# The order of Strassen splits, and two weight splits on GpSimd, in a two-block fp32 network on one core

## The reference

```python
x = x + 0.5 * swiglu(rmsnorm(x, ffn1_norm[l]), ffn1_w_gate[l], ffn1_w_up[l], ffn1_w_down[l])
...  # gated MLP with spatial gating beside a gated delta rule, w_out
x = x + 0.5 * swiglu(rmsnorm(x, ffn2_norm[l]), ffn2_w_gate[l], ffn2_w_up[l], ffn2_w_down[l])
...
def swiglu(x, w_gate, w_up, w_down):
    return (jax.nn.silu(x @ w_gate) * (x @ w_up)) @ w_down
```

## Time and profile before

| | |
|---|---|
| median of 3 runs | 1359.53 us (1359.14 to 1364.18) |
| the profiled execution | 1361.13 us, its span 1359.3 us |
| TensorE matmul busy | 1326.7 us (98% of the span) |
| VectorE, ScalarE, GpSimd busy | 930.1, 814.2, 493.7 us |
| mean granted clock of TensorE | 0.991 |

### The profile page before, as it was taken

One profiled execution on the slowest core, in us unless ns is written; L12 is line 12 of the kernel. 1 busy time (PEld: TensorE's weight loads), 2 busy tenths in 40 slices (PEclk: granted clock), 3 DMA queues, 4 the chain that ended last, 5 costly groups with the idle time before them and its releaser, 6 DMA issues.

```text
span 1359.3 us, 18294 instructions
## 1 busy us (share of the span) xinstructions
PE 1326.7 (98%) x7252; PEld 1113.8 (82%) x7252; DVE 930.1 (68%) x1162; ACT 814.2 (60%) x1095; POOL 493.7 (36%) x220
## 2 busy tenths in 40 slices
PE   9998999999999999999999999999999999999897
PEld 8887777888887888887888887788888888888786
DVE  6778886955577896687886559754335632567887
ACT  7646467456654557655567787667434654654663
POOL 1623213473641504532314231035525524462320
PEclk9999999999999999998999999999999999999999
DMA  9587884234568796577784645355854544648783
GB/s 342 187 211 249 236 288 154 97 97 164 204 163 232 217 266 227 185 183 253 203 289 155 229 175 194 121 182 177 290 183 155 198 143 148 208 156 212 242 211 109
DMA packets 42279, 269.66 MB, mean 198 GB/s; under 512 B 6321, under 2 KB 6865, under 8 KB 11217
## 3 DMA queue, kind: packets, MB, share of 16 engines
q1 hardware_dynamic: 35680, 226.69, 47.5%
q0 software_dynamic: 4608, 33.56, 13.1%
q10 hardware_dynamic: 1904, 8.23, 1.7%
HBM read 267.38 MB, written 1.08 MB: 197 GB/s over the span
## 4 chain that ended last, share of the span: by engine, by line
PE 47%; DVE 4%; POOL 4%; issue 3%; DMA 1%; ACT 1%; POOLq 0%; DVEq 0%; ACTq 0%
PE acc L394 9%; PE acc L396 9%; PE acc L395 9%; PE acc L409 6%; PE acc L410 3%; POOL forms L1010 2%; DVE wlo L375 2%; PE acc L2821 2%; DMA raw<-in_t_ffn_down 1%; POOL forms L1017 1%; PE acc L2822 1%; PE work L657 1%; PE work L658 1%; PE work L659 1%; PE work L1172 1%
## 5 line engine op out<-in xcount | busy, mean ns | idle before, releaser
L375 DVE TENSOR_TENSOR wlo<-raw,whi 128x2048 fp32r<-128x2048 f32 (+1 forms) x189 | 443.4, 2349 | 125.4 <-ACT whi L370 125.0
L370 ACT ACTIVATE whi<-raw 128x2048 fp32r<-128x2048 f32 (+1 forms) x245 | 459.8, 1886 | 102.1 <-DMA raw<-in_t_ffn_down 74.9
L409 PE MATMUL acc<-xT,whi 128*128 128x512 f32 x1208 | 429.9, 398 | 4.2 <-DVE wlo L375 3.6
L375 POOL TENSOR_TENSOR wlo<-raw,whi 128x2048 fp32r<-128x2048 f32 x56 | 271.7, 4853 | 347.8 <-ACT whi L370 339.9
L410 PE MATMUL acc<-xT,wlo 128*128 128x256 f32 x1384 | 374.0, 281 | 0.0
L409 PEld LDWEIGHTS acc<-xT,whi 128*128 128x128 f32 x1208 | 226.9, 188 | 61.2 <-issue 7.8
L410 PEld LDWEIGHTS acc<-xT,wlo 128*128 128x128 f32 x1384 | 261.4, 189 | 6.7
L394 PE MATMUL acc<-whi,xT 128*128 128x512 f32 x416 | 168.3, 405 | 0.0
L396 PE MATMUL acc<-whi,xT 128*128 128x512 f32 x416 | 162.5, 391 | 0.0
L395 PE MATMUL acc<-wlo,xT 128*128 128x512 f32 x416 | 162.3, 390 | 0.0
L769 ACT ACTIVATE hid_hi<-work 128x256 fp32r<-128x256 f32 x88 | 33.7, 383 | 134.7 <-DVE work L867 134.7
(11 more groups left out here) (422 smaller groups left out, 2122.1 us busy)
## 6 DMA issues: line engine op xcount, KB each, us to landing
raw<-in_t_ffn_up SPq DMA_DIRECT2D x85, 1024.0 KB, 5.4
raw<-in_t_m_in SPq DMA_DIRECT2D x52, 1024.0 KB, 5.2
raw<-in_t_ffn_down SPq DMA_DIRECT2D x32, 1024.0 KB, 5.6
raw<-in_t_ffn_down POOLq DMA_DIRECT2D x32, 1024.0 KB, 9.3
raw<-in_t_m_os SPq DMA_DIRECT2D x8, 1024.0 KB, 4.8
raw<-in_t_ffn_down SPq DMA_DIRECT2D x8, 512.0 KB, 7.2
raw<-in_t_m_out SPq DMA_DIRECT2D x4, 1024.0 KB, 5.2
sum_rows<-row_scratch ACTq DMA_DIRECT2D x4, 1024.0 KB, 5.1
```

Source lines behind the costliest of these rows:

```text
L370: act.activation(granule(whi, u, i), granule(raw, u, i), ACT.Copy).then_inc(hi_ready, 1)
L375: eng.tensor_tensor(granule(wlo, u, i), granule(raw, u, i), granule(whi, u, i).bitcast(F32), ALU.subtract).then_inc(lo_signal(g)[0], 1)
L409: pe.matmul(to, hi[:, c], both_parts(kt), start=first, stop=False)
```

## The change

Six edits, all in the four FFNs and the final norm:

1. The products of group 0 come in another order (P4, P2, P3, P6, P1, P7, P5); group 1 keeps its own. The first product that needs a form is now P3 at place 15; the one that needs none, P2, is at 13. The blocks summed by transfer now go to places 15, 19, 21 and 23 instead of 15, 17, 19 and 23.
2. VectorE splits a product's granule from place 15 on four places ahead, at the end of a step, instead of three ahead within it. Up pieces and blocks keep their place, so steps that had a product's split between `row` and `product` have none there now.
3. Places 18 and 29, both up pieces, are split by GpSimd: 18 after `sum_hidden(1, 0)` and ahead of `add_to_slot(21)`, 29 after `add_to_slot(32)`.
4. `add_to_slot(19)` goes ahead of `sum_hidden(1, 0)` in GpSimd's queue.
5. `rest_forms` moves on VectorE from the start of steps 10 and 25 to the end of steps 12 and 25; `round_forms(0)` moves on ScalarE from step 9 to step 10.
6. The first part of the final norm's work on VectorE (`finish_front`) moves into step 37 of the last FFN, ahead of the last product's add.

```diff
-PRODUCTS = ("P4", "P6", "P3", "P7", "P1", "P2", "P5")
+PRODUCTS = (("P4", "P2", "P3", "P6", "P1", "P7", "P5"), ("P4", "P6", "P3", "P7", "P1", "P2", "P5"))
...
+SPLIT_BY_GPSIMD = (18, 29)
...
-                if name == "P6":
+                if name in ("P6", "P3"):
                     pe.wait_ge(forms_split, 2 * (2 * f + group + 1))
...
-            if n == 9:
+            if n == 10:
                 round_forms(0)
...
-            elif n % 2 == 0 or n >= LATE_FROM:
+            elif n not in SPLIT_BY_GPSIMD and (n % 2 == 0 or n >= LATE_FROM):
                 split_lo(dve, *place(f, n))
+
+        def is_early_product(n):
+            return n > 13 and n in LATE and LATE[n][0] == "product"
+
+        def lo_of_rows(n):
+            if n <= PLACES and not is_early_product(n):
+                lo(n)
+
+        def lo_of_product(n):
+            if is_early_product(n):
+                lo(n)
 
         for n in range(5, PLACES):
             entry = LATE.get(n, ("up", n))
-            if n in (10, 25):
-                rest_forms((10, 25).index(n))
...
                 join(m)
                 row(m)
-                lo(n + 3)
+                lo_of_rows(n + 3)
                 product(m)
                 rest_hidden(m)
+                lo_of_product(n + 4)
+                if n in (12, 25):
+                    rest_forms((12, 25).index(n))
             elif entry[0] == "product":
-                if n < 38:
-                    lo(n + 3)
+                lo_of_rows(n + 3)
                 add_product(n, *entry[1:])
-            elif n < 37:
-                lo(n + 3)
-            elif n == 37:
-                lo(n + 3)
+                lo_of_product(n + 4)
+            else:
+                lo_of_rows(n + 3)
+                lo_of_product(n + 4)
+            if n == 37:
+                if f == 3:
+                    finish_front(dve)
...
         add_to_slot(15)
-        add_to_slot(17)
+        add_to_slot(19)
         sum_hidden(1, 0)
-        add_to_slot(19)
+        split_lo(pool, *place(f, 18))
+        add_to_slot(21)
         add_to_slot(23)
         sum_hidden(1, 1)
         make_forms()
         add_to_slot(30)
         add_to_slot(32)
+        split_lo(pool, *place(f, 29))
         add_to_slot(34)
         add_to_slot(38)
...
+    def finish_front(dve):
+        dve.wait_ge(final_rows_loaded, 32)
+        dve.wait_ge(resid_done, 2 * B_OUT - 1)
+        for t in range(NT):
+            dlink(dve.tensor_tensor(out_tile[:, t, FRONT], x[:, t, FRONT], gfinal2_row[:, FRONT], ALU.mult))
+        dve.wait_ge(sq_done, 2 * B_OUT + 1)
+        dlink(dve.tensor_scalar(ms[:, :], ss[:, :, 0], 1.0 / D, EPS, ALU.mult, ALU.add))
+        dwait(dve)
+        dve.sem_inc(S["out_steps"], 1)
```

More of the change, by code:

```diff
@@ L71 @@
 LATE_FROM, PLACES = 10, 40
+SPLIT_BY_GPSIMD = (18, 29)
 def late_places():
-    products = [("product", group, name) for group in range(2) for name in PRODUCTS]
+    products = [("product", group, name) for group in range(2) for name in PRODUCTS[group]]
     places = [("up", 10)]
-    for k in range(len(PRODUCTS)):
+    for k in range(7):
         places += [products[k], ("up", 11 + k)]
@@ L174, in build @@
     first_of = [units[f"ffn{f}.up0"].g for f in range(4)]
-    split_in_late_place = {first_of[f] + n for f in range(4) for n in LATE}
+    late_split_by_vector = {first_of[f] + n: n not in SPLIT_BY_GPSIMD for f in range(4) for n in LATE}
     added = {first_of[f] + n for f in range(4) for n, entry in LATE.items()
@@ L299, in lo_signal @@
     def lo_signal(g):
-        by_vector = [n for n in range(g + 1) if n % 2 == 0 or n in split_in_late_place]
+        by_vector = [n for n in range(g + 1) if late_split_by_vector.get(n, n % 2 == 0)]
         if g in by_vector:
@@ L637, in product_index @@
     def product_index(group, name):
-        return len(PRODUCTS) * group + PRODUCTS.index(name)
+        return 7 * group + PRODUCTS[group].index(name)
     def product_bank(group, name):
@@ L643, in products_so_far @@
     def products_so_far(f, group, name):
-        return 2 * len(PRODUCTS) * f + product_index(group, name) + 1
+        return 14 * f + product_index(group, name) + 1
     BACK_OF_X = pair(0)
@@ L3171, in scaled @@
                               ALU.mult).then_inc(S["out_steps"], 1)
[L3173 to L3180, removed]
         residual_out(0)
```

## The result

The changed kernel takes 1389.38 us (median of 4 runs, 1388.78 to 1390.02) against 1359.57 for the kernel before on the same chip: a ratio of 1.0215, 95% interval 1.0196 to 1.0234. Forecast were 1377 us and a range of 1363 to 1385: the direction is right, the time lies above the range. The profiled span grew from 1359.3 to 1386.8 us, by 27.5 where the working has 17.7.

What follows compares the result with a forecast made beforehand. TensorE was taken as the bound (8.38 us a pair), VectorE nearly a second (8.0). FFN terms +3.4, +4.8, +5.5, +4.9 make +18.6; less 0.9 tail, +17.7: profiled 1361.13 becomes 1378.8, median 1377 us, range 1363 to 1385.

Steps and rivals of the forecast that it cites:

- The old wait at 19 goes: TensorE's wait for `wlo` ahead of place 19, 15.9 us in 8 waits, disappears because transfer 19 is issued sooner.
- The wait at place 15: TensorE waits for group 0's forms at place 15: 2.3 us, 3.8 in the first FFN.
- place 15's weight arrives as before: Place 15's summed weight keeps its old timing, with ScalarE rounding it at 592.62 to 594.54 in the third FFN.
- Turns by whole instructions: VectorE and GpSimd alternate on SBUF by whole instructions; GpSimd's split of 29 blocks `form_lo` for 3.1 us (0 to 4.6).
- Transfer 21: Third FFN: issued behind GpSimd's split of 18 at 613.5; VectorE waits 3.2 us ahead of split 21.
- lands at 622.8 by the 9.32 of rows 3: Transfer 21 was priced at the 9.32 us that place 19's transfer took in the kernel before.
- Half clock after place 28: TensorE's resumption after the place 28 wait costs 1.67 us of half clock in each FFN (0 to 2.73).
- From there to place 37, and the tail: Place 28 to 37 keeps its old 33.08 us; moving `finish_front` takes 0.9 us off the tail (0 to 1.5).
- No block: Rival: GpSimd's split of 29 does not block `form_lo`; TensorE waits 2.7 us at place 28; about 1358 us, chance 0.09.
- The clock holds: Rival: block without half clock, 1.7 to 2 us less in each FFN, 1370 us; chance 0.12 including the shorter chain.
- a chain 2 us shorter: Same rival's other half: the chain reaches step 20 about 2 us sooner, transfer 21 landing in less than 9.3; 1370 us.
- Faster: Rival: the wait at 19 goes and nothing replaces it; worth 23.5 us, 1336 us, half of it 1348; chance 0.11.

Runs made afterwards that it cites:

- `b_swap`: Kernel before with one line moved, transfer 19 issued ahead of GpSimd's sum of the second group: 1335.88 us, ratio 0.9829.
- `hold17`: Changed kernel with SyncE's plain load of place 17 held until transfer 15 has landed: 1383.80 us, ratio to before 1.0191.
- `bs29_end`: `b_swap` with place 29 split by GpSimd and group 1's `form_lo` at the end of step 25: 1364.45 us, ratio to before 1.0037.
- `no29`: Changed kernel with place 29's split back on VectorE: 1379.40 us, ratio to before 1.0146.
- `late29`: Changed kernel with GpSimd's split of 29 held until both `form_lo` are done: 1379.43 us, ratio to before 1.0153.
- `ahead`: Kernel before with transfer 19 ahead of the sum, `finish_front` in step 37 and products split four places ahead: 1353.78 us, ratio 0.9955.
- `b_reorder`: Kernel before with group 0's reordering alone, transfer 19 still behind the sum: 1366.93 us, ratio 1.0055.
- `no18`: Changed kernel with place 18's split back on VectorE: 1373.02 us, ratio to before 1.0098.

## Why the prediction was right in kind and too low

- **The old wait at 19 goes**: right, and its worth too: 23.3 us in `b_swap`, 23.5 with the tail worked out.
- **The wait at place 15**: right place and cause; 3.1 to 4.4 us where 2.3 (3.8 in the first FFN) was forecast. The step "place 15's weight arrives as before" failed: its transfer took 10.4 us in the third FFN, not 8.7, and `hold17` shows that on the mean of the FFNs most of such an excess is the plain load of 17, and that holding it back is worth 5.6 us in all.
- **Turns by whole instructions**: right. GpSimd's split of 18 stood behind VectorE's of 17, `form_lo` behind GpSimd's of 29 for 3.0 us (forecast 3.1), and `bs29_end` shows the upper bound, nearly the full 4.85. In `no29` and `late29`, where no GpSimd instruction runs beside it, `form_lo` takes 1.22; no run shows it passing a running one. What the Trainium skill (SBUF — State Buffer, Who interferes with whom) says of the later instruction being fully blocked agrees with these rows.
- **Transfer 21**: issued behind GpSimd's split as forecast, 1.3 us later than forecast, but "lands at 622.8 by the 9.32 of rows 3" failed: 11.25. The 9.32 comes from a transfer whose next plain load was issued 2.0 us behind it; here the load of 22 was issued with it. The two transfers are the first mis-sized term. With them step 20 ends at 58.7, not 55.5, and place 28 comes at 84.5, 85.0, 85.9 and 85.8 us after product 11, where 84.6 and three times 83.0 were forecast: 7.6 us of the missing 11.4. In the first FFN the hit is luck: place 15's wait was 3.1 us instead of 3.8, as its transfer took 8.9 where the row of the kernel before has 9.9, and transfer 21 with 10.9 made up for it. The range had half a microsecond in each FFN for the load of 17, and nothing for transfer 21.
- **Half clock after place 28**: 2.6 us each instead of 1.67, the second mis-sized term: 44.1 us for the four stretches from place 28 to 30 against four times 10.05, 3.9 us in all. Its upper bound of 2.73 was named and was the better value. That the new wait is longer than the old ones (5.1 against 3.2 to 4.0 in the views) is not shown to be the reason: the 2.73 stood after the shortest of the old four, and after 5.3 to 6.2 in `bs29_end` the pair took 9.8 to 10.9.
- **From there to place 37, and the tail**: as forecast (from place 30 to 37 it is 24.7 us in each FFN, and 33.08 less 8.38 is 24.70; the tail gave 1.3 against 0.9, within its 0 to 1.5).

7.6 and 3.9 make 11.5 of the missing 11.4. None of the three rivals holds. "No block" is refuted by the 4.18 us half of `form_lo`; its 2.7 us wait "too short to halve the clock" would not have been safe either, as in `no29` waits of 2.3 us at place 28 were followed by half clock in two FFNs (10.1 us). "The clock holds" is refuted by 0.72 to 0.77, and its other half, a chain 2 us shorter, by 58.7. "Faster" was half true: the moved line is worth what that rival says, and the other edits together gave it back and 30 us more. My sum did not price the edits one by one; `ahead` shows that splitting four ahead by itself costs 18 us once TensorE is no longer held up by something else. The interaction is large: the reordering costs 7.5 us on the kernel before and 29.7 on top of the rest, and the split of 18 gains in one order and costs in the other.

Open stays what makes transfer 15 take 8.2 us in one FFN or kernel and 9.8 in another without a load of 17 beside it, whether the load of 22 alone is what made transfer 21 late, and what decides how long the half clock lasts.

## What to carry to other kernels

When a late transfer is the one thing that an almost fully busy engine waits for, move its issue ahead in its queue, alone, and measure before anything else is added: one moved line was worth 23 us here, and five further edits cost 54. Work handed to an idle engine isn't free: it takes the shared SBUF access for twice as long (4.6 against 2.2 us), it delays whatever is behind it in that engine's queue, and it inherits the waits of whatever is ahead of it. Whether it pays depends on what stands behind it: with a transfer nobody waits for behind the split of 18, the hand-over did not hurt; with transfer 21 there, it cost 16 us. A transfer's duration isn't a constant either; price one by what will start beside it.

## What the runs showed of the hardware

- A VectorE instruction with both inputs in SBUF that meets a running GpSimd instruction waits it out: 5.87 instead of 1.22 us in `bs29_end`, begun 0.08 us into 4.85 us of GpSimd. The other way too: in the changed kernel GpSimd's split of 18, 4.6 us otherwise, took 6.58 behind VectorE's.
- The time of a 1 MB transfer that adds onto SBUF depends on what starts beside it. From issue to landing it took 7.9 to 8.5 us in the changed kernel with nothing issued in its first 7 us (place 19), 8.0 to 8.4 in `b_reorder` with a second summing transfer 2.4 us behind it and the next plain load 5.4 us, 9.3 to 10.2 in the kernel before with a load 2.0 us behind it (place 19), and 10.8 to 11.2 in the changed kernel with a plain load issued with it (place 21). The second of two such transfers took 12.6 to 13.6 us in `b_reorder` and 15.7 to 16.1 in the changed kernel. The median of all 32 is 10.6 in the kernel after, 9.3 in the kernel before, 8.9 in `b_swap` and 9.1 in `no18`.
- TensorE's clock did not follow the length of the wait alone. After a wait of 3.05 us (place 15, first FFN of the changed kernel) the next pair took 8.48 us, at full clock; in `hold17` a wait of 1.95 us at place 15 of the second FFN was followed by this window:

```profile
415.01:425.00 9.99, 9.97 (x44) 8.36 (x45) 9.05 (x9) 3.16 (x4) 9.79 (x2) 0.83 0.57 156
```
